# First weight slab loaded and split ahead of the input x in a fused three-block transformer kernel

## The reference

```python
h = rms_norm(x, norm_mix_g[0])
proj = h @ a_w_in[0]        # 1024 -> 1736 columns: q, c, qi, ki, wi
```

## Time and profile before

| What | Value |
|---|---|
| Median of 3 runs | 1186.0 us (1185.4 to 1186.12) |
| Profiled execution, its own time | 1183.83 us |
| Span of the profiled execution, first to last instruction | 1182.0 us |
| PE (TensorE matmul) busy | 1163.4 us, 98% |
| DVE (VectorE) busy | 977.1 us, 83% |
| ACT (ScalarE) busy | 709.8 us, 60% |
| Mean granted TensorE clock | 0.998 |

### The profile page before, as it was taken

One profiled execution on the slowest core, in us unless ns is written; L12 is line 12 of the kernel. 1 busy time (PEld: TensorE's weight loads), 2 busy tenths in 40 slices (PEclk: granted clock), 3 DMA queues, 4 the chain that ended last, 5 costly groups with the idle time before them and its releaser, 6 DMA issues.

```text
span 1182.0 us, 25632 instructions
## 1 busy us (share of the span) xinstructions
PE 1163.4 (98%) x9126; PEld 1114.5 (94%) x9126; DVE 977.1 (83%) x1781; ACT 709.8 (60%) x1109; POOL 34.7 (3%) x64
## 2 busy tenths in 40 slices
PE   9999999999999999999999999999999999999997
PEld 7989999999899999999999999999999899999996
DVE  7877999888998898889888799999996667665666
ACT  6567656556546456556555577888866456544453
POOL 0000000000100010000000000000000000000000
PEclk9999999999999999999999999999999999999999
DMA  7535676664766786756665437457545556655551
GB/s 281 179 112 179 209 236 233 225 222 153 243 233 229 274 287 234 261 190 237 220 207 191 166 109 249 144 189 190 171 159 198 186 187 213 198 190 182 193 179 36
DMA packets 73041, 235.73 MB, mean 199 GB/s; under 512 B 7424, under 2 KB 16640, under 8 KB 72848
## 3 DMA queue, kind: packets, MB, share of 16 engines
q1 hardware_dynamic: 64304, 203.86, 51.6%
q0 software_dynamic: 8528, 30.98, 7.6%
q10 hardware_dynamic: 144, 0.02, 0.0%
HBM read 233.73 MB, written 1.09 MB: 199 GB/s over the span
## 4 chain that ended last, share of the span: by engine, by line
PE 82%; DVE 11%; issue 4%; ACT 3%; DVEq 1%; ACTq 0%
PE ps L202 25%; PE ps L203 24%; PE ps L204 24%; PE ps L234 3%; DVE w_lo L194 3%; PE ps L235 2%; DVE arena L1962 2%; ACT w_hi L189 1%; DVE arena L892 1%; DVE arena L1950 1%; PE ps L1627 0%; DVE arena L927 0%; DVE arena L1944 0%; DVE arena L455 0%; DVE arena L924 0%
## 5 line engine op out<-in xcount | busy, mean ns | idle before, releaser
L202 PE MATMUL ps<-a_hi,w_hi 128*128 128x256 f32 x1656 | 469.4, 283 | 2.4 <-DVE w_lo L194 1.6
L194 DVE TENSOR_TENSOR w_lo<-w_raw,w_hi 128x1024 fp32r<-128x1024 f32 x381 | 461.1, 1218 | 10.7 <-ACT w_hi L189 4.9
L203 PE MATMUL ps<-a_lo,w_hi 128*128 128x256 f32 x1656 | 462.5, 279 | 0.0
L204 PE MATMUL ps<-a_hi,w_lo 128*128 128x256 f32 x1656 | 462.3, 279 | 0.0
L189 ACT ACTIVATE w_hi<-w_raw 128x1024 fp32r<-128x1024 f32 x381 | 390.7, 1048 | 23.0 <-PE ps L204 12.5
L202 PEld LDWEIGHTS ps<-a_hi,w_hi 128*128 128x128 f32 x1656 | 311.4, 188 | 8.3 <-issue 4.6
L203 PEld LDWEIGHTS ps<-a_lo,w_hi 128*128 128x128 f32 x1656 | 311.5, 188 | 0.7 <-issue 0.2
L204 PEld LDWEIGHTS ps<-a_hi,w_lo 128*128 128x128 f32 x1656 | 311.4, 188 | 0.0
L202 PE MATMUL ps<-b_both,w_hi 128*128 128x256 f32 x560 | 158.1, 282 | 1.7 <-DVE b_both L952 0.9
L204 PE MATMUL ps<-b_both,w_lo 128*128 128x256 f32 x560 | 156.3, 279 | 0.0
L203 PE MATMUL ps<-b_both,w_hi 128*128 128x256 f32 x560 | 156.3, 279 | 0.0
(11 more groups left out here) (315 smaller groups left out, 1681.9 us busy)
## 6 DMA issues: line engine op xcount, KB each, us to landing
w_raw<-stream SPq DMA_DIRECT2D x381, 512.0 KB, 3.9
arena<-ada POOLq DMA_DIRECT2D x48, 512.0 KB, 6.0
c_both<-cum_rows POOLq DMA_DIRECT2D x4, 1024.0 KB
arena<-x SPq DMA_DIRECT2D x2, 512.0 KB, 4.4
con<-consts SPq DMA_DIRECT2D x1, 1024.0 KB, 5.7
arena<-row_cols POOLq DMA_DIRECT2D x2, 512.0 KB
arena<-c_rows POOLq DMA_DIRECT2D x1, 512.0 KB, 4.1
out<-arena SPq DMA_DIRECT2D x2, 256.0 KB, 2.2
```

The lines of the kernel that those rows point to most:

```text
L194: dve.tensor_tensor(w_lo[:, s % RING], w_raw[:, s % RING], w_hi[:, s % RING].bitcast(F32), ALU.subtract).then_inc(w_lo_ready, 1)
L202: pe.matmul(o, wh, xh, start=start, stop=False, skip_group_check=shared)
L203: pe.matmul(o, wh, xl, start=False, stop=False, skip_group_check=shared)
L204: return pe.matmul(o, wl, xh, start=False, stop=stop, skip_group_check=shared)
```

## The change

Three things change places; nothing is added or taken away.

1. SyncE issues slab 0 right behind the small constant and ahead of both halves of `x`. The wait for the second half of `x` ahead of slab 1 stays where it was.
2. ScalarE splits slab 0 ahead of all eight high parts of `x`, which then follow each other.
3. VectorE makes slab 0's low part ahead of all eight low parts of `x`, which then follow each other.

```diff
-            for m in range(4):
-                high(m)
             split_hi(act, 0)
-            for m in range(4, NT):
+            for m in range(NT):
                 high(m)
             split_hi(act, 1)
...
             dve.wait_ge(par_in, 16)
-            for m in range(4):
-                lower(m)
             split_lo(dve, 0)
-            for m in range(4, NT):
+            for m in range(NT):
                 lower(m)
             split_lo(dve, 1)
...
             sp.dma_start(con[:, 0:P], consts[:, 0:P]).then_inc(small_in, 16)
+            sp.dma_start(w_raw[:, 0], stream[0]).then_inc(w_landed[0], 16)
             x_rows = x.rearrange("(b p) d -> p b d", p=P)
             sp.dma_start(x_tok[:, :, 0:DM // 2], x_rows[:, :, 0:DM // 2]).then_inc(x_in, 16)
             sp.dma_start(x_tok[:, :, DM // 2:DM], x_rows[:, :, DM // 2:DM]).then_inc(x_in_2, 16)
...
-            load(0)
             sp.wait_ge(x_in_2, 16)
             load(1)
```

## The result

The changed kernel takes 1187.16 us, the median of 18 runs (1185.19 to 1189.25), against 1185.53 us for the kernel before in 18 runs (1183.8 to 1186.42). The ratio is 1.0016, 95% interval 1.0009 to 1.0023: slower by about 1.9 us, which is under the 2.37 us (0.2%) that the prediction calls no change. The medians themselves are 1.63 us apart, the fastest runs 1.39. The profiled execution took 1185.56 us, 1.73 more than that of before.

A forecast was written before the change was run, and what follows sets the result against it. The run was taken as bound by TensorE (chain 82% PE), its start a race between the split line and slabs 1 and 2 arriving. Overlapping terms left the largest, +0.85 us: 1186.0 + 0.9 = 1186.9 us, range 1185.3 to 1189.4.

The forecast's parts named there:

- The splits cost nothing in front: ACT and DVE, before x: slab 0's splits fill idle time, removing 1.07 us of ACT and 1.24 of DVE from the line.
- x lands one place later: DMA at the start: x's halves move one place down, the first landing at 6.67, the second at 7.85.
- T: Landing time of x's second half in the changed kernel, forecast 7.85 us, bounds 7.4 to 8.35.
- ACT's line is unchanged, TensorE's is 0.4 longer: Behind x: ACT's high parts end at 10.5, about as before; TensorE's first real matmul comes at 10.65 instead of 10.26.
- Slabs 1 and 2 decide: Later issue behind x's wait: TensorE starts slab 1 0.6 us later at 13.75, slab 2 0.85 later at 16.8.
- +0.85 us at slab 2: TensorE's start of slab 2, at 16.8 instead of 15.96; the largest of overlapping terms, taken as the whole loss.
- the upper bound of +1.35: Whole-run loss if x's second half lands as late as 8.35 us.
- Nothing gives it back: Rest of the run: attention work starts from TensorE's products and the chain stays on compute, so the +0.85 us remains.
- The later clock: Rival, chance 0.27: TensorE's idle gap before x delays its clock's rise, costing up to +3.6 us (1189.6).
- the rise between transposes and dummies: Case of the clock rival: transposes at the lower clock, dummies at the higher; first real matmul at 12.0, +1.75 us.
- The faster arrival without loss: Rival, chance 0.15: slab 1 takes 2.7 us from issue and is ready at 12.55; no change, 1186.0.
- the reorder doesn't act: Rival, chance 0.03: slab 0 lands late, high parts start 0.4 us late under the 0.85; time as forecast.

The follow-up runs named there:

- e3: Changed kernel without SyncE's wait for x's second half ahead of slab 1; ratio 1.0008 [0.9999, 1.0018] to the kernel before.
- e8: Changed kernel without the wait ahead of slab 1 and the dummies behind x's transposes, one more dummy matmul ahead of x; ratio 0.9993 [0.9985, 1.0002].
- e6: Changed kernel with one more dummy matmul ahead of x, to fill TensorE's idle time; ratio 1.0005 [0.9996, 1.0013] to the kernel before.
- e10: Changed kernel with one more dummy matmul ahead of x, run again; ratio 1.0011 [1.0002, 1.0020] to the kernel before.
- e1: Kernel before with only slab 0's load moved ahead of x, both splits left in place; ratio 1.0013 [1.0004, 1.0022].
- e9: The changed kernel run again, with no further edit; ratio 1.0016 [1.0007, 1.0025] to the kernel before.
- e7: Changed kernel without the wait ahead of slab 1 and without the dummies behind x's transposes; ratio 0.9999 [0.9989, 1.0008] to the kernel before.
- e5: Changed kernel with SyncE's wait ahead of slab 1 moved on to the last low part of x; ratio 1.0042 [1.0029, 1.0055].
- e4: Kernel before without SyncE's wait for x's second half ahead of slab 1, old order kept; ratio 1.0001 [0.9992, 1.0010].
- e2: Changed kernel with slab 0 loaded behind x again, so only the splits go first; ratio 1.0015 [1.0006, 1.0024] to the kernel before.

## Why the prediction was right, point by point

**The splits cost nothing in front.** Right. ACT began slab 0 at 5.43 (5.2 forecast; it waited for the gains, which landed last), and the high parts were not held up: they waited 1.01 us for the transposes.

**x lands one place later.** Right in kind: slab 1's issue, which waits for x's second half, came at 8.02, so T was 8.0 and not 7.85, inside the bounds 7.4 to 8.35.

**ACT's line is unchanged, TensorE's is 0.4 longer.** Right. High parts 7.50 to 10.5, as worked out. TensorE's second matmul came 0.33 later. e3, where no slab is waited for, puts TensorE's line at +0.54; e8 shows that it was the dummies behind x, as the working had it.

**Slabs 1 and 2 decide.** Right in mechanism, low in size. The step that was too small is the term "+0.85 us at slab 2". Slab 1 started at 13.91 (13.75 forecast). Slab 2 was taken to move by T - 6.64 = 1.2 us, from 13.2 to 14.4; it landed at 8.88 + 6.14 = 15.02. Of the 0.6 missing, 0.2 are SyncE's later issue (8.88 - 7.50 = 1.38) and 0.45 a longer flight, 6.1 us against 5.7. So +1.45 instead of +0.85, just past the upper bound of +1.35, because the bound moved x's landing alone and held the flight fixed. The flight was not the same length in each profile of this order: slab 2's split started at 15.04 here, at 15.30 and 15.12 in e6 and e10, but at 14.04 in e1 and 14.54 in e9. By the arrival alone slab 2 would have been some 0.45 late in e1 and 0.9 in e9. So the size of this term varies between executions, and what sets it is not shown.

**Nothing gives it back.** Right. The timelines of DVE follow the shift through the run by the low parts of slabs. In the kernel before, the 41st slab and the last two:

```profile
151.30 1.22 DVE L194 TENSOR_TENSOR w_lo<-w_raw,w_hi 128x1024 fp32r<-128x1024 f32 x1
...
1161.29 2.35 DVE L194 TENSOR_TENSOR w_lo<-w_raw,w_hi 128x1024 fp32r<-128x1024 f32 x2
```

And in the changed kernel:

```profile
152.80 1.22 DVE L194 TENSOR_TENSOR w_lo<-w_raw,w_hi 128x1024 fp32r<-128x1024 f32 x1
...
1163.00 2.35 DVE L194 TENSOR_TENSOR w_lo<-w_raw,w_hi 128x1024 fp32r<-128x1024 f32 x2
```

So +1.50 at 150 us and +1.71 at the end. At slab 2 and in the fastest runs the shifts agree within 0.3 us in all but four of the twelve rows of the table. In those (e1, e6, e7, e10) the profile had the shift larger by 0.4 to 0.7; in e1 and e7 the profile also holds the clock's fall, which the fastest run need not.

**The rivals.** The later clock happens: e9 shows it in the changed kernel, so one of the signs of being wrong, transposes 0.21 apart past 8.3, came true in one of its two profiles. e9 is the case of the working with the rise between transposes and dummies: +1.75 worked out, and +1.53 measured at slab 2, 0.6 past the arrival of that execution. The cost of the clock is bare once the arrival is mended (e7). Where the working was wrong is that the gap "can only delay the rise": in e1, e5 and e7 the granted clock read 1.00 from 6.9 to 7.7, with transposes 0.1 us apart, and 0.50 from 8.7 to 11.1. Nor does the gap always cost the clock: of the six profiles with 1.58 to 1.97 us of idle TensorE ahead of x, four (e1, e5, e7, e9) had the lower clock behind it and two (the changed kernel's first, e3) did not. The faster arrival without loss didn't happen; it needs the wait removed. That the reorder doesn't act is refuted by rows above.

**The rule on issuing early.** The Trainium skill (DMA: Bandwidth & Descriptors, Rules for kernel authors) says to issue a DMA early and wait late, and the runs agree: taking away the one wait for x ahead of slab 1 is worth 0.9 us in e3, and in the old order nothing in e4.

**The measured time.** 1186.9 was forecast and 1187.16 measured, but from different starts: the three runs shown of before had a median of 1186.0, 18 runs have 1185.53. The measured change, 1.9 [1.1, 2.7], is twice the forecast 0.9. That the two times lie within 0.3 us is luck: a start 0.5 too high hides half of a change that came out too small. (The low end of the range is 0.1 under its own sum, 1186.0 - 0.6 = 1185.4.)

## What to carry to other kernels

Before a transfer is put in front of others, look at which wait hangs on the last of those others: it now ends later, and with an empty queue behind it, so that the transfers that follow pay their whole flight in the open. Take such a wait away, or put it on an earlier transfer, in the same edit. And when a load moves, check whether TensorE is left idle where its operand used to arrive: behind such a gap it may run on at the lower clock.

## What the runs showed that was not expected

The kernel's time spreads by 2.6 to 4.1 us between runs (1183.58 to 1187.08 over 35 runs of the kernel before), up to twice the change. Profiles show three places for it, all far behind the change. Between 140 and 280 us, matmuls go at one of two paces in an execution. These windows of PE (busy and count, granted clock, DMA share, GB/s) are of the kernel before and of e4, at the same granted clock:

```profile
160.00:240.00 80.00, 80.00 (x688) 1.00 0.68 229
```

```profile
160.00:240.00 80.00, 80.00 (x682) 1.00 0.67 228
```

That is 0.9% of some 130 us, about 1.2 us. e1, e3, e4 and e8 had the slower pace, the changed kernel and the others the faster. At about 833 us TensorE idled 0.35 us in 830 to 836 in the kernel before (5.65 of 6.00 busy), and 1.71 us in the same stretch of e10 (4.29 of 6.00 in 831.5 to 837.5). And in e1 and e2 the clock fell near 70 us (mean 0.62 and 0.64 from 69.5 to 74), where the changed kernel's stayed at 1.00. What chooses the pace is open. For a change of 1 us the start of a slab in the profile and the fastest of many runs agree better than medians do.
